# Activation blocks rounded one block later through a doubled scratch, and gains, bias row and p laid out by DMA: one decoder layer on one core

## The reference, cut to what matters

```python
h = h + 0.5 * swiglu(rmsnorm(h, ffn1_norm), ffn1_w_gu, ffn1_w_down)     # F = 2816
h = h + hybrid_mixer(rmsnorm(h, mix_norm), w_in, ..., w_out, rel_bias)
h = h + 0.5 * swiglu(rmsnorm(h, ffn2_norm), ffn2_w_gu, ffn2_w_down)
h = h + sigmoid(rmsnorm(h, ple_norm) @ w_ple_gate) * (p @ w_ple_proj)   # p: 256 x 256
out = rmsnorm(h, final_norm)

def rmsnorm(x, g): return x * rsqrt(mean(x * x) + EPS) * g
def swiglu(x, w_gu, w_down):
    gate, up = split(x @ w_gu)
    return (silu(gate) * up) @ w_down
```

## Time and profile before

| | |
|---|---|
| three runs | 537.56, 537.82, 539.17 us, median 537.82 |
| profiled execution | 537.52 us, its span 535.3 us |
| TensorE clock granted | 0.996 over the span |
| TensorE busy | 521.9 us (97%), 2475 matmuls |
| VectorE busy | 327.6 us (61%) |
| ScalarE busy | 271.9 us (51%) |
| POOL busy | 77.8 us (15%) |
| DMA moved | 112.02 MB, mean 209 GB/s |

### The profile page before, as it was taken

The page is one execution under the profiler, slowest core; times in us unless marked ns, Lnnn a source line. Parts: engine busy times, 40 slices in busy tenths (PEclk is TensorE's granted clock), DMA queues, the critical chain, the costliest instruction groups (busy, mean ns, idle before and its releaser), DMA issues.

```text
span 535.3 us, 6918 instructions
## 1 busy us (share of the span) xinstructions
PE 521.9 (97%) x2475; PEld 424.1 (79%) x2475; DVE 327.6 (61%) x434; ACT 271.9 (51%) x336; POOL 77.8 (15%) x144
## 2 busy tenths in 40 slices
PE   8999999999988999999999999999999999999994
PEld 5788888888776888877777788888888888888883
DVE  3683655845628474455799586656666557374675
ACT  4953354433616384876153766354533454453736
POOL 1503222222210210000000000222222222010000
PEclk9999999999999999999999999999999999999998
DMA  8995877859567968341245286777678757368202
GB/s 257 367 364 186 274 236 258 265 155 303 167 229 225 388 191 318 118 131 66 80 157 173 75 283 220 213 240 249 197 226 283 251 181 244 134 232 274 80 0 78
DMA packets 78166, 112.02 MB, mean 209 GB/s; under 512 B 5408, under 2 KB 51184, under 8 KB 78016
## 3 DMA queue, kind: packets, MB, share of 16 engines
q1 hardware_dynamic: 71472, 93.34, 53.2%
q0 software_dynamic: 6512, 18.32, 10.4%
q10 hardware_dynamic: 160, 0.07, 0.0%
HBM read 103.82 MB, written 9.45 MB: 212 GB/s over the span
## 4 chain that ended last, share of the span: by engine, by line
PE 65%; DMA 18%; DVE 6%; issue 5%; ACT 3%; POOL 2%; SPq 0%; DVEq 0%; ACTq 0%; POOLq 0%
PE acc L545 60%; DMA act_in<-act_dram 8%; DMA act_dram<-act_sq 7%; PE side L545 3%; POOL act_in L488 2%; DMA raw<-in_ffn_w_gu 2%; PE turn L585 2%; ACT w_hi L909 2%; DVE w_lo L1195 2%; DMA h<-in_x 1%; DVE act_sq L1272 1%; DVE AT L1463 1%; DVE act L1262 0%; DVE w_lo L1496 0%; PE turn L545 0%
## 5 line engine op out<-in xcount | busy, mean ns | idle before, releaser
L1195 DVE TENSOR_TENSOR w_lo<-raw,w_hi 128x2048 fp32r<-128x2048 f32 (+1 forms) x87 | 192.1, 2214 | 60.9 <-ACT w_hi L909 60.8
L545 PE MATMUL acc<-w_hi,hT_hi 128*128 128x512 f32 x496 | 196.1, 395 | 0.2 <-DVE w_lo L1195 0.2
L545 PE MATMUL acc<-w_hi,hT_lo 128*128 128x512 f32 x496 | 193.3, 390 | 0.0
L545 PE MATMUL acc<-w_lo,hT_hi 128*128 128x512 f32 x496 | 193.2, 389 | 0.0
L909 ACT ACTIVATE w_hi<-raw 128x2048 fp32r<-128x2048 f32 (+1 forms) x87 | 160.0, 1851 | 30.5 <-PE acc L545 28.2
L545 PEld LDWEIGHTS acc<-w_hi,hT_hi 128*128 128x128 f32 x496 | 93.1, 188 | 21.9 <-issue 1.8
L545 PEld LDWEIGHTS acc<-w_hi,hT_lo 128*128 128x128 f32 x496 | 93.1, 188 | 19.6
L545 PEld LDWEIGHTS acc<-w_lo,hT_hi 128*128 128x128 f32 x496 | 93.2, 188 | 18.5
L950 ACT ACTIVATE a_hiT<-act_in 128x512 f32 (+1 forms) x22 | 13.9, 632 | 132.5 <-DMA act_in<-act_dram 132.5
L545 PE MATMUL acc<-w_hi,a_hiT 128*128 128x512 f32 x176 | 68.9, 391 | 3.1 <-DVE w_lo L1195 1.7
L545 PE MATMUL acc<-w_hi,a_loT 128*128 128x512 f32 x176 | 68.5, 389 | 0.0
(11 more groups left out here) (171 smaller groups left out, 340.6 us busy)
## 6 DMA issues: line engine op xcount, KB each, us to landing
raw<-in_ffn_w_gu SPq DMA_DIRECT2D x82, 512.0 KB, 5.0
raw<-in_ffn_w_down SPq DMA_DIRECT2D x40, 512.0 KB, 5.5
raw<-in_w_in SPq DMA_DIRECT2D x24, 512.0 KB, 6.5
act_dram<-act_sq POOLq DMA_DIRECT2D x22, 256.0 KB, 4.2
act_in<-act_dram POOLq DMA_DIRECT2D x88, 64.0 KB, 4.2
raw<-in_w_out SPq DMA_DIRECT2D x8, 512.0 KB, 4.3
raw<-in_w_ple_gate SPq DMA_DIRECT2D x8, 512.0 KB, 5.0
raw<-in_ffn_w_gu SPq DMA_DIRECT2D x10, 256.0 KB, 6.2
```

What stands on the lines that cost most here:

```text
L545: return nc.tensor.matmul(o, lhsT, rhs, start=start, stop=stop, skip_group_check=True)
L1195: V.tensor_tensor(w_lo[:, slot, :nk * N], raw[:, slot, :nk * N], w_hi[:, slot, :nk * N].bitcast(F32), ALU.subtract).then_inc(lo_ready, 1)
```

## The change

1. `act_dram` and `act_in` have two buffers, `act_sq` stays single. POOL's waits look two blocks back in place of one. ScalarE and VectorE round block b-2 at the end of block b (blocks 1 and 2 stand ahead of the loop, which has 4 rounds in place of 5); block 9's rounding stands at k = 1 of the down part and block 10's at k = 3.
2. The gains are loaded column by column, one of 4 bytes at a time, straight into `gains`; transpose, copy and their waits are gone.
3. The bias row is built in DRAM: 24 DMAs, one for each bucket, write `turned_row` (256 distances by 8 heads); when all have landed, one DMA copies it turned into `row_dram`, 4 bytes at a time, and another adds the causal part. The matmul, the addition of `causal` and the DMA of `bias_row` are gone. All of it stands in POOL's queue ahead of the first round trip.
4. `p` takes the same round trip as an activation block: transposed by VectorE at k = 2 of the second down part, a 12th `act_turn`, rounded at k = 5. `p_turn` is gone.
5. In `DVE_STEPS`, `lv0` is split into its two halves, with `pv0` between them.

```diff
-DVE_STEPS = [..., "lo43", "lv0", "pv0", "pt1.0", ...]
+DVE_STEPS = [..., "lo43", "lv0.0", "pv0", "lv0.1", "pt1.0", ...]
...
-        act_in = at("act_in", 50, [P, N])
+        act_in = at("act_in", 50, [P, 2, N])
...
-        act_dram = nc.dram_tensor("act_dram", [P, N], F32).ap()
+        act_dram = nc.dram_tensor("act_dram", [2, P, N], F32).ap()
+        turned_row = nc.dram_tensor("turned_row", [T, MH], F32).ap()
...
             def act_turn(g):
                 pool.wait_ge(act_turned, g + 1)
-                if g:
-                    pool.wait_ge(act_back, 64 * g)
-                pool.dma_start(act_dram, act_sq[:]).then_inc(act_out, 16)
+                if g >= 2:
+                    pool.wait_ge(act_back, 64 * (g - 1))
+                pool.dma_start(act_dram[g % 2], act_sq[:]).then_inc(act_out, 16)
                 pool.wait_ge(act_out, 16 * (g + 1))
-                if g:
-                    pool.wait_ge(act_lo, g)
+                if g >= 2:
+                    pool.wait_ge(act_lo, g - 1)
                 for j in range(4):
...
-            for k, g in enumerate([mix_norm, ffn2_norm, ple_norm]):
-                pool.dma_start(gain_rows[k * KC:(k + 1) * KC, :], g.rearrange("a (c p) -> (a c) p", p=P)
-                               ).then_inc(gains_in, 16)
-            pool.dma_start(rel[:], rel_bias).then_inc(bias_in, 16)
-            pool.dma_start(rows[:], bucket_rows).then_inc(bias_in, 16)
-            pool.dma_start(causal[:], causal_row).then_inc(bias_in, 16)
+            with nc.allow_non_contiguous_dma(reason="one gain a partition"):
+                for k, g in enumerate([mix_norm, ffn2_norm, ple_norm]):
+                    pool.dma_start(gains[:, (k + 1) * KC:(k + 2) * KC], g.rearrange("a (c p) -> p (a c)", p=P)
+                                   ).then_inc(gains_in, 16)
+            for bucket, near, far in bucket_runs():
+                pool.dma_start(turned_row[T - far:T - near, :],
+                               bass.AP(tensor=rel_bias.tensor, offset=bucket * MH, ap=[[0, far - near], [1, MH]])
+                               ).then_inc(bias_in, 16)
+            pool.wait_ge(bias_in, 16 * len(bucket_runs()))
+            with nc.allow_non_contiguous_dma(reason="one bias a distance and head"):
+                pool.dma_start(row_dram[:, 0:T].unsqueeze(2), turned_row.rearrange("t h -> h t").unsqueeze(2)).then_inc(row_out, 16)
+            pool.dma_start(row_dram[:, T:], causal_row[:, T:]).then_inc(row_out, 16)
             pool.wait_ge(zeroed, 2)
             pool.dma_start(gk_up[0:LR, :], w_gk_up).then_inc(small_in, 16)
...
             for b in range(NB):
                 act_turn(b)
-            pool.wait_ge(side_dve, SIDE["bias_row"][2])
-            pool.dma_start(row_dram, bias_row[:]).then_inc(row_out, 16)
-            pool.wait_ge(row_out, 16)
+            pool.wait_ge(row_out, 32)
             pool.dma_start(skew_dram, ...).then_inc(skew_out, 16)
...
             for b in range(NB):
                 act_turn(NB + b)
+            act_turn(2 * NB)
             h_turn(1)
...
-                        if f == 1 and n == 0 and k == 2:
-                            p_turn()
-                        if f == 0 and n == 0 and k == 1:
-                            o = side_open("gain")
-                            pe.wait_ge(gains_in, 48)
-                            flip(o[:, 0:3 * KC], gain_rows[:], 3 * KC).then_inc(side_done, 1)
-                            o = side_open("bias_row")
-                            pe.wait_ge(bias_in, 48)
-                            mm(o[0:MH, 0:BIAS_W], rel[:], rows[:], True, True).then_inc(side_done, 1)
...
                     sp_(1)
-                    if j:
-                        act_part(f, b - 1)
+                    if j and not (isinstance(b, int) and b == 1):
+                        act_part(f, b - 2, (j + NB * f) % 2)
                 blk(0, 0)
-                with act_e.Fori(0, (NB - 1) // 2) as i:
+                for b in (1, 2):
+                    blk(b, b)
+                with act_e.Fori(0, (NB - 3) // 2) as i:
                     for j in range(2):
-                        blk(i * 2 + (1 + j), 1 + j, i)
+                        blk(i * 2 + (3 + j), 3 + j, i)
                 for n in range(2):
                     for k in range(6):
                         u = U_DOWN[f] + 6 * n + k
-                        if n == 0 and k == 2:
-                            act_part(f, NB - 1)
+                        if n == 0 and k in (1, 3):
+                            b = NB - 2 + k // 2
+                            act_part(f, b, (b + NB * f) % 2)
+                        if f == 1 and n == 0 and k == 5:
+                            act_part(1, NB, 0, pT_hi[:])
...
-                            o = side_of("gain")
-                            V.tensor_copy(gains[:, KC:], o[:, 0:3 * KC]).then_inc(side_dve, 1)
-                            o = side_of("bias_row")
-                            V.tensor_tensor(bias_row[:], o[0:MH, 0:BIAS_W], causal[:], ALU.add).then_inc(side_dve, 1)
+                            dve.wait_ge(gains_in, 48)
...
                         if f == 1 and n == 0 and k == 2:
-                            dve.wait_ge(turn_hi, hi_count["p"] + 1)
-                            V.tensor_tensor(pT_lo[:].rearrange("p c t -> p (c t)"), turn[:, TURN["p"] % 2, :], ...)
+                            dve.wait_ge(ple_in, 32)
+                            act_squares(1, NB, p_nat)
+                        if f == 1 and n == 0 and k == 5:
+                            act_part(1, NB, 0, pT_lo[:], pT_hi[:])
```

More of the change, by code:

```diff
@@ L12 @@
+import math
 from contextlib import ExitStack
+import numpy as np
 import concourse.bass as bass
@@ L147, in plan_turns @@
     add("h2.1", 2)
-    add("p")
     add("h3.1", 2)
@@ L157, in plan_side @@
 def plan_side():
-    uses = [("gain0", "dve"), ("gain", "dve"), ("bias_row", "dve")]
+    uses = [("gain0", "dve")]
     for at in sorted(MIX):
@@ L174, in plan_side, with bucket_of, bucket_runs @@
     return out
+def bucket_of(dist):
+    exact = BUCKETS // 2
+    if dist < exact:
+        return dist
+    large = np.log(np.float32(dist) / np.float32(exact)) / np.float32(math.log(4096 / exact)) * np.float32(BUCKETS - exact)
+    return min(exact + int(large), BUCKETS - 1)
+def bucket_runs():
+    runs = []
+    for dist in range(T):
+        if runs and runs[-1][0] == bucket_of(dist):
+            runs[-1][2] = dist + 1
+        else:
+            runs.append([bucket_of(dist), dist, dist + 1])
+    return runs
 TURN, TURN_AT = plan_turns()
@@ L869, in _ @@
                 acc_free(B)
-                pe.wait_ge(turn_read, turned("p"))
+                pe.wait_ge(act_lo, 2 * NB + 1)
                 unit(u, u % RING, B % 2,
@@ L1248, in h_part, with act_part @@
                             op0=ALU.mult, op1=ALU.subtract).then_inc(h_lo, 1)
-            def act_part(f, b):
+            def act_part(f, b, par, lo=None, hi=None):
                 dve.wait_ge(act_hi, b + (NB * f + 1))
-                out = a_loT[:, bass.ds(b * 2, 2), :].rearrange("p j (m i e) -> p (j m) i e", m=M, i=4)
-                hi = a_hiT[:, bass.ds(b * 2, 2), :].rearrange("p j (m i e) -> p (j m) i e", m=M, i=4)
-                V.tensor_tensor(out, act_in[:].rearrange("p (i k e) -> p k i e", i=4, k=4), hi.bitcast(F32),
+                if lo is None:
+                    lo, hi = a_loT[:, bass.ds(b * 2, 2), :], a_hiT[:, bass.ds(b * 2, 2), :]
+                V.tensor_tensor(lo.rearrange("p j (m i e) -> p (j m) i e", m=M, i=4),
+                                act_in[:, par, :].rearrange("p (i k e) -> p k i e", i=4, k=4),
+                                hi.rearrange("p j (m i e) -> p (j m) i e", m=M, i=4).bitcast(F32),
                                 ALU.subtract).then_inc(act_lo, 1)
@@ L1296, in blk @@
                     act_squares(f, b)
-                    if j:
-                        act_part(f, b - 1)
+                    if j and not (isinstance(b, int) and b == 1):
+                        act_part(f, b - 2, (j + NB * f) % 2)
                 blk(0, 0)
-                with dve.Fori(0, (NB - 1) // 2) as i:
+                for b in (1, 2):
+                    blk(b, b)
+                with dve.Fori(0, (NB - 3) // 2) as i:
                     for j in range(2):
-                        blk(i * 2 + (1 + j), 1 + j, i)
+                        blk(i * 2 + (3 + j), 3 + j, i)
                 for n in range(2):
@@ L1481, in _ @@
                     n += 4
-                elif name == "p" or name[:2] == "pv" or name[:3] == "T_o":
+                elif name[:2] == "pv" or name[:3] == "T_o":
                     n += 1
```

47 lines of the change are left out of this document (18 added, 29 removed), and 2 rows, old and new, of the table DVE_STEPS.

## The result

The changed kernel takes 562.13 us (median of four runs, 557.29 to 564.42) against 537.69 (535.87 to 539.17) for the kernel before on the same chip: a ratio of 1.044, 95% interval 1.037 to 1.052. It is 24 us slower; the forecast was 531.9 and its range ended at 535.6. The profiled execution took 563.5 us, its span is 561.5.

What follows compares the result with a forecast made beforehand. TensorE was taken as the bound, busy in 97% of the span, with removable gaps: A to E sum to 6.11, less 0.2 for small runs gives 5.9, so 537.52 becomes 531.6, median 531.9; range 531 to 533, with rivals 531.0 to 535.6.

Steps and rivals of the forecast that it cites:

- A: First FFN's down part: the gap for the norm columns' transpose and the bias matmul on TensorE goes, 1.11 us.
- B: First FFN's down part: the last unit of n=0 no longer waits for the rounding of block 10, 1.65 us.
- C: First FFN's down part: the next unit no longer waits for its weights' low part, 1.98 us.
- D: Second FFN: the gap for the transposes of p on TensorE goes, 0.45 us.
- E: Mixer: with pv0 rounded between lv0's halves, TensorE's second pt1 transposes no longer wait for oT_lo, 0.92 us.
- Issue costs: POOL's queue at the start: 1.04 us a gains DMA, 0.51 a bucket, 1.57 the turned row.
- The gains at 8 ns a run: Norm loads while unit 4's weights come in: 192 runs an engine cost nothing at 8 ns, 1.0 us at 17.4.
- the price of a 4-byte run of the turned row: Turning DMA before block 0's send: 8 ns a run taken from lrw, 17.4 from above; 2.0 to 4.5 us.
- The second rival: Before block 4: at 58 ns a run or more the kernel is slower, 550 us at 100 ns; chance 0.08.
- The signs that the prediction named for being wrong: A gap before block 4 or unit 4 behind block 0's late send, or that send issued later than 43 us.
- the change leaves the clock alone: TensorE's clock is at full grant (1.00, 2.4 GHz) all through, and nothing in the change alters that.
- the buckets' landing of 5.5 to 6.3: Start of POOL's queue: the last bucket, issued at 32.0, lands 5.5 to 6.3 us later, at 37.5 to 38.3.

Runs made afterwards that it cites:

- few_runs: The changed kernel with one DMA of 256 32-byte runs for the 24 bucket DMAs and a turning copy of eight 1 KB runs; 530.96 us, ratio 0.989.
- double_only: The kernel before with part 1 of the change alone (two buffers for act_dram and act_in, rounding one block later); 533.95 us without one run, ratio 0.993.
- row_long_runs: The changed kernel with the turning DMA copying the same 8 KB in order as eight runs of 1 KB; 537.65 us, ratio 1.000 to the kernel before.
- one_bucket_dma: The changed kernel with one DMA of 256 runs of 32 bytes for the 24 bucket DMAs, the turning DMA kept; 544.72 us, ratio 1.010 to the kernel before.
- bucket_sbuf: `row_long_runs` with the 24 bucket DMAs written to one partition of SBUF, then one DMA to the row in DRAM; 531.25 us, ratio 0.987 to the kernel before.

## Why the prediction was wrong

**A to E held.** The sum of 6.11 came out as 6.2 in the changed kernel, and as 4.78, 1.07 and 0.51 (6.36) in `few_runs`. Reading gaps between starts, less the steps they contain, was right within 0.15 us for A to C together, for D and for E. B and C go with part 1 alone (`double_only`), as the prediction said.

**Issue costs held.** 0.9 a gains DMA in place of 1.04, 0.50 a bucket, 1.64 for the turned row against 1.57. The gains at 8 ns a run cost nothing seen.

**The step that failed is the price of a 4-byte run of the turned row**: "I take 8 ns, because lrw is the row with the same shape and count", with 17.4 as the upper bound. It measured 23.5 us for the row where 2.0 to 4.5 were forecast: 92 ns a run if 8 engines share them, 76 with a plain copy's landing taken off. The second rival had the place, its mechanism (each run its own write to DRAM) and nearly the price: 550 at 100 ns. It got 0.08, because the upper bound came from packets of loads to SBUF, some 200 bytes each in the mean (0.02 MB in 103 packets). Both bounds were rows of another target, and "above" was no bound for this one. The signs that the prediction named for being wrong all came: the gap before block 4 behind a late send, a gap before unit 4, and the send issued at 49.80, later than 43.

The rival itself fell short by 12 us, or 13.5 of the profiled execution (563.5 against 550). That is the wait before block 3 (4.78), which it did not have, the half clock behind both waits (5.22), where the prediction held that the change leaves the clock alone, 3.24 more at block 4 (21.74 in place of 18.5) and unit 4's 0.45. In its chain the row started at 45.52 and not at 40, and the send landed 11.1 us behind the row (69.0 to 80.1) and not 2.7. The same send took 9.3 us in `row_long_runs` too; why it is slow there no run shows. From that landing to TensorE's restart it took 4.0 us, as forecast.

**A second step failed unseen**: the buckets' landing of 5.5 to 6.3, taken from `rel` and the round trip. It was 13.9, and the forecast had no case in which it stops the weights. `rel` is 1.0 KB and goes to SBUF; a bucket of 32 bytes to DRAM had no row of its size and target, and the range of the others was lent to it. This is the wait before block 3: 4.78 + 2.95, and unit 4's 0.45.

**Third**, the text asked only how long small runs hold POOL's queue. `one_bucket_dma` shows that they hold the weight loads too, down to 4 GB/s.

## What to carry to other kernels

A DMA price is a price for its target, its run length and its number of engines; if no row of the trace shares all three, there is no upper bound, and the rival that costs ten times more deserves a real chance. Tiny writes to DRAM were paid here by the weight loads of another queue: keep them out of stretches where a stream of loads has nothing in reserve, or reorder the data in SBUF on an engine that is idle. A layout change of 8 KB can outweigh four sound improvements, so time it alone.

## What the runs showed of the hardware

- 2048 runs of 4 bytes from DRAM to DRAM landed in 23.5 us with 8 as outermost dimension, in 10.6 with 256 and another order of addresses, and in 11.3 to 8 partitions of SBUF. While they were written to DRAM, all traffic of the core fell to 4 GB/s (`one_bucket_dma`, 36 to 40 us).
- A DMA of one 32-byte run counted 32 packets, as did one of 256 runs. 24 single-run DMAs to DRAM cut the traffic to 55 GB/s in the stretch 32 to 36 us, while 24 of 16 whole 32-byte runs left it at 351, and `bucket_sbuf`, with 16 single-run DMAs among its 24 to SBUF, at 292.
- After a wait of 21.97 us TensorE's granted clock was 0.50 and stayed there for 4.8 us of matmuls; after the one of 5.01 us it stood at 0.50 until 54.6, 6.1 us. In `row_long_runs`, behind a wait of 4.80 us, the grant was 0.57 over 48 to 52 us and 1.00 after.
